# A fused two-block transformer kernel on one core: where the squares of the hidden layer stand in two engine queues, eight multiplications on another engine, and the order of a few loads and stores

## The chip, the cores and the metric

The program runs on one core of one Trainium2 chip. The metric is device time in microseconds (us) of one execution, as a median over runs; shorter is better.

## What is computed

The input x is 1024 tokens by 1024 features, float32. Three stages follow each other.

```python
# block 1: two layers, each x = x + rms_norm(mixer(rms_norm(x)))
#   layer 0: gmlp mixer (three 1024 x 2048 projections, 128-token spatial gating)
#   layer 1: dilated window attention, three groups of 16 heads
# block 2, on 1024 + 16 (meta) tokens:
#   h = rms_norm(x); z = h @ w_in
#   o = [stick-breaking attention | state-space scan (Ssd) | gated recurrence (Hgrn)]
#   x = x + o @ w_out
#   h = rms_norm(x)
#   u = relu(h @ w_up) ** 2
#   x = x + u @ w_down          # w_up: 1024 x 4096
```

The two recurrences work on chunks of 128 tokens and carry a state from one chunk to the next.

## The kernel before

Every large product is made three times on TensorE (PE), from operands that are split into an upper part (`hi`, rounded) and a rest (`lo`). ScalarE (ACT) makes `hi` (`split_hi`, L137), VectorE (DVE) makes `lo` (`split_lo`, L142), and PE then runs 24 matmuls for one weight unit of 1024 x 128 on 512 tokens (`products`, L155). SyncE (SP) loads the units into two raw buffers (L132). Each engine works through its own list of instructions in the order written; waits between engines are semaphores. GpSimd (POOL) mostly issues transfers.

**The last stage, `output_and_mlp`.** `units` is a list of 144 weight units: 8 of the output projection (positions 0 to 7), then for the first 512 tokens `up` and `down` in turn, 8 of each (up at positions 8 to 15, 24 to 31, 40 to 47, 56 to 63), the output projection of the second 512 tokens at 68 to 75, the rest of the first half, and last the same `up` and `down` units for the second 512 tokens. At each position n:

- PE: the recurrence phase n-1; wait for `lo` of unit n; wait until unit n-2 has left its bank; 24 matmuls into `z[n % 2]`.
- DVE: `split(n + 1)`; recurrence phase n-1; if unit n-1 was an up unit, `h_lo` of it (L4030); then the exit of unit n (for an up unit L4039: relu times the inverse norm, into `m[n % 2]`; for a down unit L4041: added to x).
- ACT: `split(n + 1)`, which waits until PE is done with unit n-1; recurrence phase n-1; `hidden(n - 1)`: if unit n-1 was an up unit, two squares of its `m` (L3924 `h_hi`, L3925 `y`).

The recurrence phases are 28 of `Ssd` (0 to 27: 4 chunks of 7), then 32 of `Hgrn` (28 to 59: 4 chunks of 8) and one last. Of an Hgrn chunk, phase 0 makes the gate's logarithms (ACT `mag`, `soft`; DVE sums to `cum`), phase 1 the distances (14 small DVE operations, L3751 and L3752), phase 2 their exponential on ACT (L3699) and on DVE `dq`, `dk` (L3760, L3761), `kend` (L3763) and `qe` (L3766). Phases 3 to 6 are scores on PE (L3648), which wait for `dq` and `dk`, and a masked sum on DVE; phase 7 gives the output. The chunk's inputs come to `raw` by `hg.load` (L3611 to L3616, two transfers from POOL's queue). `hg.load(0)` is issued at the stage's start; `sd.pool` stores each Ssd chunk's output (L2344) and ends with a wait for all four stores. The tile `dist` lies over the tile of Ssd's output, so DVE's first phase 1 waits for those stores (`ssd_stored`).

**The seam between attention and block 2.** x + y * norm * gain is made for the first 512 tokens at the end of `dilated_attention`, and for the second 512 at the start of `projection_and_sticks`, one 128-feature row k at a time. There DVE runs `scaled(k)` (L2978: m = y * inv), `add(k)` (L2982: x), `lower(k)` (L2988: the `lo` part) and for each two rows `pair` (L2994: the sum of two squares). ACT makes `hi` (L2716) and the square (L2718). PE runs 12 matmuls of row k for the first two weight units, and for each pair a matmul with ones (L2854) that sums over the features. In attention, `next_y(k)` (L2227), `next_x(k)` (L2233), `next_lower(k)` do the same, among DVE's `split_lo` of units that PE waits for (L1908).

**The stage boundary after the projection.** SP loads the first two units of w_out into the raw buffers, then stores the last projected unit (L2690). The next stage (`gated_recurrence`, the first Hgrn chunks) reads that unit.

Of the kernel before, what the change touches and what calls it, by code (L numbers as in the profile page):

```python
# [17 lines left out]
ACT = mybir.ActivationFunctionType  # L18
# [3 lines left out]
P = 128  # L22
# [1213 lines left out]
def dilated_attention(nc, shared, a_in, w, hi, lo, x_kept, yo, over_yo, over_w, blocks, inv, inv_post, x_out, bias_dram, o_dram, lse_dram, lead, lead_sum, ident,  # L1236
# [13 lines left out]
    with Stage(nc, "da") as st:  # L1250
# [246 lines left out]
        def _(pool):  # L1497
# [31 lines left out]
            for n in range(1, turns + 1):  # L1529
                turn(n)  # L1530

# [417 lines left out]
        def _(dve):  # L1949
# [272 lines left out]
            def next_y(k):  # L2222
                if k == 0:
                    dve.wait_ge(s_y, 16)
                    dve.wait_ge(s_ydone, 1)
                wait(dve, s_yx, k - 1)
                nc.vector.tensor_tensor(ym[k % 2], yo[:, k, halves[0]], inv_post[:, halves[0]], ALU.mult).then_inc(s_ym, 1)  # L2227

# [20 lines left out]
            for j in range(8, 24):  # L2249
                ahead = rows_of.get(j, ()) if j > 18 else ()  # L2250
                for k in ahead:
                    next_y(k)
# [7 lines left out]
                for k in rows_of.get(j, ()):  # L2260
                    if not ahead:
                        next_y(k)
# [251 lines left out]
def projection_and_sticks(nc, shared, mix_norms, late_out, a, w, hi, lo, inv, x, x_again, x_out, over_x, heads, hg, keep, table, cst, proj, conv, o_cat, ident, ones):  # L2514
# [31 lines left out]
    with Stage(nc, "pr") as st:  # L2546
# [19 lines left out]
        pairs = [total[:, 0:HALF], total[:, HALF:T]]  # L2566
# [24 lines left out]
        (s_par, s_table, s_m, s_xp, s_hi, s_lo, s_sq, s_pair, s_pmm, s_ln, s_inv, s_eps, s_zero, s_zout) = (  # L2591
            st.sem(n) for n in ("par", "table_in", "m_s", "xp", "hi_s", "lo_s", "sq_s", "pair", "pair_mm", "ln_s", "inv_s", "eps_s", "zero_s", "zero_out"))
# [29 lines left out]
        def _(sp):  # L2622
# [77 lines left out]
        def _(pool):  # L2700
            pool.wait_ge(s_zout, 48)
# [10 lines left out]
        def _(act):  # L2712
            nc.scalar.preload_act_table_set(EXP_LN)
            for k in range(KT):
                act.wait_ge(s_xp, k + 1)
                nc.scalar.activation(hi[:, k, late], x[:, k, late_in], ACT.Identity, scale=pre[:, k:k + 1]).then_inc(s_hi, 1)  # L2716
                wait(act, s_pair, k // 2)
# [3 lines left out]
            act.wait_ge(s_pmm, KT // 2)  # L2721
# [126 lines left out]
        def _(pe):  # L2848
            w.split(pe, 1, 0)
            w.products(begin[1][0][:, 0:PIECES[0][1]], 1, hi, lo, slice(*PIECES[0]))  # L2850

            def square_sum(p):
                pe.wait_ge(s_pair, p + 1)
                nc.tensor.matmul(pb[:, :], ones, pairs[p % 2], start=p == 0, stop=p == KT // 2 - 1).then_inc(s_pmm, 1)  # L2854

            for k in range(KT):
# [7 lines left out]
                if k and k % 2 == 0:  # L2864
                    square_sum(k // 2 - 1)
            square_sum(KT // 2 - 1)
# [103 lines left out]
        def _(dve):  # L2970
# [5 lines left out]
            def scaled(k):  # L2976
                wait(dve, s_xp, k - 1)
# [1248 lines left out]
```

## Time and profile before

| | |
|---|---|
| median of 3 runs | 3526.36 us (3518.29, 3526.36, 3527.9) |
| the profiled execution's own time | 3518.29 us |
| its span in the trace | 3516.5 us |
| mean granted TensorE clock | 0.994 of 2.4 GHz |
| busy, share of the span | PE 97%, DVE 61%, ACT 44%, POOL 3% |
| bytes moved | 315.8 MB, mean 90 GB/s |

Times in the trace are counted from the span's start. The seam lies at about 1971 to 2047, `gated_recurrence` at about 2545 to 2622, the last stage from 2623 to the end; its Hgrn phases begin at about 2819.

### The profile page before, as it was taken

To read this page: it belongs to the slowest core of one execution; us is meant where nothing else is said; L and a number is where in the kernel's file an instruction comes from. 1 tells how busy PE (TensorE), PEld (TensorE's weight loads), DVE (VectorE), ACT (ScalarE), POOL (GpSimd) and SP (SyncE) were. 2 spreads that over 40 slices of the span, in tenths; PEclk is the share of its full clock that TensorE was granted. 3 is DMA by queue.
4 is the path that set the end of the run, shared out by engine and by line. 5 is a ranking of instruction groups with operands and counts; after the bars stand their busy time and mean duration, and the time that the engine had idled before them with its cause. 6 is when DMAs were issued, how large, how long until landed. Compare 5 with 4: busy or idle time off the path is not lost. (4 is left out here: it accounts for less than half of the span.)

```text
span 3516.5 us, 48187 instructions
## 1 busy us (share of the span) xinstructions
PE 3420.0 (97%) x17584; PEld 2786.3 (79%) x17584; DVE 2153.6 (61%) x4253; ACT 1548.1 (44%) x3115; POOL 106.8 (3%) x143
## 2 busy tenths in 40 slices
PE   8999999989999999999999999999989999999999
PEld 6878887867777777777777788888878888878887
DVE  5477774575555566666778546776676577644333
ACT  4254443345444444544445546665334233332222
POOL 0000001000000000000000000000010000000000
PEclk9999999999999999999999999999989999999999
DMA  4232224621222122222223330122333222322223
GB/s 151 90 106 97 97 91 147 223 76 55 64 61 61 56 67 70 63 65 68 63 65 105 126 113 32 46 71 70 114 108 101 95 89 86 106 91 94 96 96 120
DMA packets 162201, 315.79 MB, mean 90 GB/s; under 512 B 33360, under 2 KB 78976, under 8 KB 161840
## 3 DMA queue, kind: packets, MB, share of 16 engines
q1 hardware_dynamic: 144048, 267.43, 23.0%
q0 software_dynamic: 15808, 36.89, 3.6%
q10 hardware_dynamic: 2112, 8.39, 0.6%
q8 instruction: 142, 2.33, 0.3%
q14 instruction: 91, 0.75, 0.1%
HBM read 259.69 MB, written 59.19 MB: 91 GB/s over the span
## 5 line engine op out<-in xcount | busy, mean ns | idle before, releaser
L137 ACT ACTIVATE all_w_hi<-all_w_raw 128x1024 fp32r<-128x1024 f32 x241 | 254.4, 1057 | 695.7 <-PE om_z L155 501.4
L142 DVE TENSOR_TENSOR all_w_lo<-all_w_raw,all_w_hi 128x1024 fp32r<-128x1024 f32 x241 | 294.9, 1224 | 246.2 <-ACT all_w_hi L137 245.9
L155 PE MATMUL om_z<-all_hi,all_w_hi 128*128 128x512 f32 x640 | 255.4, 399 | 3.3 <-PEq L45 2.0
L155 PE MATMUL om_z<-all_hi,all_w_lo 128*128 128x512 f32 x640 | 254.2, 397 | 0.0
L155 PE MATMUL om_z<-all_lo,all_w_hi 128*128 128x512 f32 x640 | 252.6, 395 | 0.0
L2128 DVE CUSTOM_DVE_ANT_0 at_logit<-da_qk,at_bias 128x256 f32<-128x256 f32 (+1 forms) x384 | 130.0, 376 | 164.3 <-issue 163.7
L1663 ACT ACTIVATE at_p<-at_logit,da_pair_max 128x256 f32<-128x256 f32 (+1 forms) x384 | 177.5, 465 | 100.3 <-DVE da_pair_max L2128 100.3
L155 PE MATMUL all_bank<-all_hi,all_w_hi 128*128 128x344 f32 (+1 forms) x632 | 215.3, 341 | 2.8 <-PEq L45 1.6
L1655 ACT ACTIVATE at_pt<-da_tr 128x512 f32<-128x512 f32 (+1 forms) x192 | 101.2, 527 | 263.6 <-PE da_tr L1855 263.5
L155 PE MATMUL om_z<-om_h_hi,all_w_hi 128*128 128x512 f32 x512 | 204.2, 399 | 2.1 <-DVE all_w_lo L142 1.6
L155 PE MATMUL all_bank<-all_hi,all_w_lo 128*128 128x344 f32 (+1 forms) x632 | 203.2, 322 | 0.0
L155 PE MATMUL all_bank<-all_lo,all_w_hi 128*128 128x344 f32 (+1 forms) x632 | 202.8, 321 | 0.0
L155 PE MATMUL om_z<-om_h_lo,all_w_hi 128*128 128x512 f32 x512 | 202.4, 395 | 0.0
L155 PE MATMUL om_z<-om_h_hi,all_w_lo 128*128 128x512 f32 x512 | 201.8, 394 | 0.0
L4041 DVE TENSOR_TENSOR all_yo<-all_yo,om_z 128x512 f32<-128x512 f32 x80 | 55.0, 688 | 194.2 <-PE om_z L155 194.1
L1865 PE MATMUL da_pv<-at_v,at_pt 128*128 128x64 f32 x1280 | 164.1, 267 | 0.0
L1865 PEld LDWEIGHTS da_pv<-at_v,at_pt 128*128 128x128 f32 x1280 | 159.8, 192 | 2.0
L2145 DVE TENSOR_TENSOR da_o<-da_pv,da_rden 128x128 f32<-128x128 f32 x192 | 56.0, 292 | 167.5 <-PE da_pv L1865 162.0
L1196 ACT ACTIVATE all_w_hi<-all_w_raw 128x512 fp32r<-128x512 f32 x190 | 118.3, 623 | 73.7 <-PE all_bank L1214 60.5
L155 PEld LDWEIGHTS om_z<-all_hi,all_w_hi 128*128 128x128 f32 x640 | 120.9, 189 | 32.3 <-issue 3.4
L155 PEld LDWEIGHTS om_z<-all_lo,all_w_hi 128*128 128x128 f32 x640 | 121.1, 189 | 27.5
L155 PEld LDWEIGHTS om_z<-all_hi,all_w_lo 128*128 128x128 f32 x640 | 120.8, 189 | 27.0
(815 smaller groups left out, 8757.0 us busy)
## 6 DMA issues: line engine op xcount, KB each, us to landing
all_w_raw<-in_w_mlp SPq DMA_DIRECT2D x128, 512.0 KB, 3.4
all_w_raw<-in_w_qkv SPq DMA_DIRECT2D x136, 256.0 KB, 2.7
all_w_raw<-in_w_ug SPq DMA_DIRECT2D x48, 512.0 KB, 4.2
all_w_raw<-in_w_in SPq DMA_DIRECT2D x27, 512.0 KB, 3.5
all_w_raw<-in_w_v SPq DMA_DIRECT2D x20, 512.0 KB, 4.4
vhat<-ag_vst ACTq DMA_DIRECT2D x4, 2048.0 KB, 7.4
ow_v<-vhat SPq DMA_DIRECT2D x16, 512.0 KB, 3.3
da_before<-o_groups POOLq DMA_DIRECT2D x32, 256.0 KB, 4.0
```

The source lines that it names most:

```text
L137: self.nc.scalar.activation(self.hi[b][:, :], self.raw[b][:, :], ACT.Copy).then_inc(self.hi_done[b], 1)
L142: self.nc.vector.tensor_tensor(self.lo[b][:, :], self.raw[b][:, :], self.hi[b][:, :].bitcast(F32), ALU.subtract).then_inc(self.lo_done[b], 1)
L155: last = self.nc.tensor.matmul(out, wp[b][:, w], ap[:, k, cols], start=(k == 0 and m == 0), stop=(k == KT - 1 and m == 2))
L1196: self.nc.scalar.activation(self.hi[n % self.slots], self.tile[name], ACT.Copy, scale=self.scales[j] if name in ("a11", "a12") else 1.0).t ...
L1655: nc.scalar.activation(pt[t % 2][:, 0:wd], tr[:, 0:wd], ACT.Copy).then_inc(s_pt, 1)
L1663: last = nc.scalar.activation(p[t % 2][:, hh, 0:wd], logit[t % 2][:, hh, 0:wd], ACT.Exp, scale=-1.0, bias=pair_max[:, t, hh:hh + 1], accum ...
L1865: last = nc.tensor.matmul(pv[:, 64 * hh:64 * hh + 64], pt[t % 2][:, i * P:i * P + P], v[:, t + x, 64 * hh:64 * hh + 64], start=(x == 0), s ...
L2128: last = nc.vector.tensor_tensor_reduce(out=logit[t % 2][:, hh, 0:wd], in0=qk[hh][:, 0:wd], in1=bias[ag][hh][x][:, :], scale=1.0, scalar=3 ...
L2145: nc.vector.tensor_tensor(o[:, t, :].rearrange("p (h c) -> p h c", h=2), pv[:, 0:P].rearrange("p (h c) -> p h c", h=2), rden[:, t, :].rear ...
L4041: nc.vector.tensor_tensor(x[:, i, halves[h]], x[:, i, halves[h]], z[b][:, :], ALU.add).then_inc(s_ev, 1)
```

## The change

Four groups of edits.

1. In the last stage ACT's two squares of an up unit move from position n + 1 to the end of position n, where they wait for the exit of that unit; they now stand ahead of `split(n + 2)`. On DVE, `h_lo` of the unit before moves ahead of `split(n + 1)` and the recurrence phase.
2. `hg.load(0)` is issued after `sd.pool`, not at the stage's start; the wait `ssd_stored` goes. In Hgrn's phase 2, `kend` and `qe` come ahead of `dq` and `dk`.
3. At both parts of the seam the product y * inv (8 rows of 128x512 each) goes from DVE to POOL. At the second part the sums of squares are no longer added in pairs with 4 matmuls but gathered by 7 DVE operations into one tile, with one matmul at the end.
4. SP stores the last projected unit before it loads the two units of w_out, not after.

```diff
@@ dilated_attention, gpsimd, after its turns
+            pool.wait_ge(s_y, 16)
+            pool.wait_ge(s_ydone, 1)
+            for k in range(KT):
+                wait(pool, s_yx, k - 1)
+                nc.gpsimd.tensor_tensor(ym[k % 2], yo[:, k, halves[0]], inv_post[:, halves[0]], ALU.mult).then_inc(s_ym, 1)
@@ dilated_attention, vector: next_y(k), the same product, and its calls go
-                nc.vector.tensor_tensor(ym[k % 2], yo[:, k, halves[0]], inv_post[:, halves[0]], ALU.mult).then_inc(s_ym, 1)
@@ projection_and_sticks, sync
+            sp.wait_ge(s_ev, 3 * NU)
+            sp.dma_start(proj[units[NU - 1]][:, P - META:], ev[(NU - 1) % 3][:, TAPS - 1:]).then_inc(late_out, 16)
             sp.wait_ge(h_next, 32)
             w.load(sp, 0, 14, a["w_out2"][0])
             w.load(sp, 1, 13, a["w_out2"][1])
-            sp.wait_ge(s_ev, 3 * NU)
-            sp.dma_start(proj[units[NU - 1]][:, P - META:], ev[(NU - 1) % 3][:, TAPS - 1:]).then_inc(late_out, 16)
@@ projection_and_sticks, gpsimd
+            for k in range(KT):
+                wait(pool, s_xp, k - 1)
+                nc.gpsimd.tensor_tensor(m[k % 2], x[:, k, late_in], inv[:, late], ALU.mult).then_inc(s_m, 1)
@@ projection_and_sticks, tensor: the four square_sum(p) go
+            pe.wait_ge(s_acc0, KT - 1)
+            nc.tensor.matmul(pb[:, :], ones, total[:, late], start=True, stop=True).then_inc(s_tot, 1)
@@ projection_and_sticks, vector
-            scaled(0)
-            scaled(1)
             add(0)
-            for k in range(KT):
-                if k + 2 < KT:
-                    scaled(k + 2)
+            lower(0)
+            add(1)
+            for k in range(1, KT):
                 if k + 1 < KT:
                     add(k + 1)
                 lower(k)
-                if k % 2:
-                    pair(k // 2)
+                gather(k)
+            def gather(k):
+                dve.wait_ge(s_sq, k + 1)
+                t = total[:, late]
+                if k == 1:
+                    nc.vector.scalar_tensor_tensor(t, sq[0], 1.0, sq[1], ALU.mult, ALU.add).then_inc(s_acc0, 1)
+                else:
+                    dve.wait_ge(s_acc0, k - 1)
+                    nc.vector.scalar_tensor_tensor(t, t, 1.0, sq[k % 2], ALU.mult, ALU.add).then_inc(s_acc0, 1)
@@ Hgrn.pool and Hgrn.dve
+        self.load(pool, 0)
-            if i == 0:
-                dve.wait_ge(*self.ssd_stored)
-            dve.wait_ge(self.s_ed, i + 1)
-            nc.vector.tensor_tensor(t["dq"], ...)
-            nc.vector.tensor_tensor(t["dk"], ...).then_inc(self.s_dqk, 1)
             dve.wait_ge(self.s_end, i + 1)
             nc.vector.tensor_tensor(t["kend"], ...)
             nc.vector.tensor_tensor(t["qe"], ...)
+            dve.wait_ge(self.s_ed, i + 1)
+            nc.vector.tensor_tensor(t["dq"], ...)
+            nc.vector.tensor_tensor(t["dk"], ...).then_inc(self.s_dqk, 1)
@@ output_and_mlp, gpsimd
-            hg.load(pool, 0)
             sd.pool(pool)
             hg.pool(pool)
@@ output_and_mlp, scalar
                 split(n + 1)
                 recurrences(lambda r: r.act, act, n - 1)
-                hidden(n - 1)
...
+                if kind == "up":
+                    act.wait_ge(s_ev, n + 1)
+                    wait(act, s_hl, ups(u) - 1)
+                    nc.scalar.activation(h_hi[:, i, :], m[n % 2][:, :], ACT.Square)
+                    nc.scalar.activation(y[n % 2][:, :], m[n % 2][:, :], ACT.Square).then_inc(s_hh, 1)
@@ output_and_mlp, vector
-                split(n + 1)
-                recurrences(lambda r: r.dve, dve, n - 1)
                 if n and units[n - 1][0] == "up":
                     v = units[n - 1]
                     dve.wait_ge(s_hh, ups(v) + 1)
                     nc.vector.tensor_tensor(h_lo[:, v[3], :], y[(n - 1) % 2][:, :], h_hi[:, v[3], :].bitcast(F32), ALU.subtract).then_inc(s_hl, 1)
+                split(n + 1)
+                recurrences(lambda r: r.dve, dve, n - 1)
```

## Rows read from the trace of the kernel before

**Rows 1.** The page: busy us (share of the span) xinstructions.

```profile
PE 3420.0 (97%) x17584; PEld 2786.3 (79%) x17584; DVE 2153.6 (61%) x4253; ACT 1548.1 (44%) x3115; POOL 106.8 (3%) x143
```

**Rows 2.** PE's waits, 2623 to 3516: waiter <- releaser: us, times, longest.

```profile
PE om_two L3648 <- DVE x_kept L3761: 3.5, 4, 0.9
...
PE om_z L155 <- DVE om_h_lo L4030: 0.5, 1, 0.5
```

**Rows 3.** The chain that ended last, 2806 to 2838: start, us, what.

```profile
2806.98 22.31 PE om_z L155 x96
...
2836.14 2.05 PE om_two L3648 x16
```

**Rows 4.** ACT's timeline, 2818 to 2832: start, us, instruction [idle before].

```profile
2818.25 1.06 ACT L137 ACTIVATE all_w_hi<-all_w_raw 128x1024 fp32r<-128x1024 f32 x1 [2.09 <-PE om_z L155]
...
2820.94 0.62 ACT L3925 ACTIVATE om_y<-om_m 128x512 f32<-128x512 f32 x1
...
2830.34 1.69 ACT L3699 ACTIVATE hi_f<-hi_f 128x1792 f32<-128x1792 f32 x1
```

**Rows 5.** DVE's timeline, 2815 to 2833.

```profile
2815.87 0.69 DVE L2480 TENSOR_TENSOR hi_f<-hi_f,mixers_gn 128x512 f32<-128x512 f32 x1
...
2819.34 1.23 DVE L142 TENSOR_TENSOR all_w_lo<-all_w_raw,all_w_hi 128x1024 fp32r<-128x1024 f32 x1 [0.46 <-ACT all_w_hi L137]
2820.54 0.43 DVE L3731 SCALAR_TENSOR_TENSOR x_kept<-om_raw,x_kept 128x256 f32<-128x256 f32 x1
...
2822.32 0.67 DVE L4030 TENSOR_TENSOR om_h_lo<-om_y,om_h_hi 128x512 fp32r<-128x512 f32 x1
2823.75 0.69 DVE L4039 SCALAR_TENSOR_TENSOR om_m<-om_z,all_inv 128x512 f32<-128x512 f32 x1 [0.76 <-PE om_z L155]
...
2826.04 0.28 DVE L3751 TENSOR_TENSOR hi_f<-x_kept 128x128 f32<-128x128 f32 x1
...
2828.87 0.69 DVE L4030 TENSOR_TENSOR om_h_lo<-om_y,om_h_hi 128x512 fp32r<-128x512 f32 x1
...
2832.12 2.03 DVE L3760 TENSOR_TENSOR hi_f<-hi_f,om_raw 128x1792 f32<-128x1792 f32 x1 [0.43 <-ACT hi_f L3699]
```

**Rows 6.** Transfers, 2500 to 3070: KB each, median us from issue to landing.

```profile
om_raw<-proj POOLq DMA_DIRECT2D x8, 256.0 KB, 4.8
...
o_cat<-hi_f POOLq DMA_DIRECT2D x4, 256.0 KB, 2.5
```

**Rows 7.** POOL's timeline at the start of the last stage.

```profile
2625.53 1.48 POOL L3616 DMA_DIRECT2D om_raw<-proj  x2
```

**Rows 8.** POOL's timeline in the stage before the last.

```profile
2580.11 1.98 POOL L3330 TENSOR_TENSOR hg_gg<-hg_gate,mixers_hg_gn 128x256 f32<-128x256 f32 x1 [8.22 <-ACT hg_gate L3398]
2585.61 0.73 POOL L3333 TENSOR_TENSOR x_kept<-hg_o,hg_gg 128x256 f32<-128x256 f32 x1 [3.53 <-ACT hg_o L3367]
```

**Rows 9.** DVE's timeline at the same time.

```profile
2579.48 2.02 DVE L3533 TENSOR_TENSOR hg_dq<-hg_dist,hp_raw 128x1792 f32<-128x1792 f32 x1
2581.42 2.55 DVE L3535 TENSOR_TENSOR hg_dk<-hg_dist,hp_key 128x1792 f32<-128x1792 f32 x1
```

**Rows 10.** Lines of the seam: count, ns min/median/max, first and last start.

```profile
L2982 DVE SCALAR_TENSOR_TENSOR all_yo<-pr_big,mixers_post,da_y x8: 744/745/748, 2023.7 to 2037.8; 128x512 f32<-128x512 f32 x8
...
L2854 PE MATMUL pr_pb<-pr_total,all_ones x8: 590/591/592, 2033.0 to 2045.4; 128*128 128x512 f32 x8
```

**Rows 11.** Waits, 1970 to 2050.

```profile
PE all_bank L1908 <- DVE all_w_lo L142: 2.4, 2, 1.5
```

**Rows 12.** SP's timeline ahead of the stage boundary.

```profile
2525.84 1.18 SPq L132 DMA_DIRECT2D all_w_raw<-in_w_out  x2
...
2542.78 0.33 SPq L2690 DMA_DIRECT2D proj<-pr_ev  x1
```

**Rows 13.** PE's waits, 2094 to 2101.

```profile
PE pr_pb L2903 <- ACT pr_ce L2746: 2.3, 1, 2.3
```

**Rows 14.** The stretch right behind that wait: length, PE, PEld, DVE, ACT, POOL busy, clock, DMA.

```profile
2097.30:2100.70 3.40, 3.40 (x12) 2.90 (x12) 0.10 (x1) 0.56 (x1) 0.00 (x0) 0.57 0.00 0
```

More of the change, by code:

```diff
@@ L2974, in _ @@
             sd.dve_start(dve)
-            def scaled(k):
-                wait(dve, s_xp, k - 1)
-                nc.vector.tensor_tensor(m[k % 2], x[:, k, late_in], inv[:, late], ALU.mult).then_inc(s_m, 1)
             def add(k):
@@ L2989, in lower @@
                                                ALU.mult, ALU.subtract).then_inc(s_lo, 1)
-            def pair(p):
-                dve.wait_ge(s_sq, 2 * p + 2)
-                wait(dve, s_pmm, p - 1)
-                nc.vector.tensor_tensor(pairs[p % 2], sq[0], sq[1], ALU.add).then_inc(s_pair, 1)
-            scaled(0)
-            scaled(1)
+            def gather(k):
[6 more added lines that the diff above has]
+                    nc.vector.scalar_tensor_tensor(t, t, 1.0, sq[k % 2], ALU.mult, ALU.add).then_inc(s_acc0, 1)
             add(0)
-            for k in range(KT):
-                if k + 2 < KT:
-                    scaled(k + 2)
+            lower(0)
+            add(1)
+            for k in range(1, KT):
                 if k + 1 < KT:
@@ L3598, with __init__ @@
     PHASES = 8
[L3600 to L3601 removed]
+    def __init__(self, st, proj, o_cat, keep, tile, bank, cst, first, count):
         self.nc, self.proj, self.o_cat, self.first, self.count = st.nc, proj, o_cat, first, count
@@ L3758, in dve @@
                 link(nc.vector.memset(t["key"][:, :, 0:P - META], 0.0))
-            dve.wait_ge(self.s_ed, i + 1)
-            nc.vector.tensor_tensor(t["dq"], t["dist"], over(t["raw"][:, 0:2, :]), ALU.mult)
-            nc.vector.tensor_tensor(t["dk"], t["dist"], over(t["key"]), ALU.mult).then_inc(self.s_dqk, 1)
             dve.wait_ge(self.s_end, i + 1)
@@ L3766, in dve @@
             nc.vector.tensor_tensor(t["qe"], t["ecum"], t["raw"][:, 0:2, :], ALU.mult).then_inc(self.s_qe, 1)
+            dve.wait_ge(self.s_ed, i + 1)
+            nc.vector.tensor_tensor(t["dq"], t["dist"], over(t["raw"][:, 0:2, :]), ALU.mult)
+            nc.vector.tensor_tensor(t["dk"], t["dist"], over(t["key"]), ALU.mult).then_inc(self.s_dqk, 1)
         if ph in (3, 4, 5, 6):
@@ L3843, in output_and_mlp @@
         sd = Ssd(st, proj, conv, o_cat, keep, sd_tile, (bank[0], bank[1], bank[2:4], bank[5]), cst, first, count)
-        hg = Hgrn(st, proj, o_cat, keep, hg_tile, (two[:, :], bank[2], bank[3], bank[4][:, 0:2 * P], bank[4][:, 2 * P:]), cst, first, count,
-                  (sd.s_left, 16 * count))
+        hg = Hgrn(st, proj, o_cat, keep, hg_tile, (two[:, :], bank[2], bank[3], bank[4][:, 0:2 * P], bank[4][:, 2 * P:]), cst, first, count)
         s_o = st.sems("o_in", tiles // 2)
@@ L3916, in scale @@
                     nc.scalar.activation(hi[:, c, halves[h]], x[:, c, halves[h]], ACT.Identity, scale=gain[:, c:c + 1]).then_inc(s_hi2, 1)
-            def hidden(n):
-                u = units[n]
-                if n < 0 or u[0] != "up":
-                    return
-                act.wait_ge(s_ev, n + 1)
-                wait(act, s_hl, ups(u) - 1)
-                nc.scalar.activation(h_hi[:, u[3], :], m[n % 2][:, :], ACT.Square)
-                nc.scalar.activation(y[n % 2][:, :], m[n % 2][:, :], ACT.Square).then_inc(s_hh, 1)
             act.wait_ge(s_gain, 16)
```

27 lines of the change are left out of this document (5 added, 22 removed).

## Prediction

> **What bounds the kernel now.** First the page's line of busy times [rows 1]: PE is busy for 97% of the span, so DVE or ACT work costs nothing while it stays behind PE's matmuls, and an edit can gain only where PE waits. So next PE's waits in the last stage [rows 2]: over 893 us only a handful of us, 3.5 of them at four places, the scores of a gated-recurrence chunk waiting for `dk`. One more, 0.5, is PE at a first down unit waiting for the `h_lo` of the last up unit. The chain [rows 3] gives PE's pace: 96 matmuls, four units, in 22.31 us, so 5.58 per unit; they end at 2829.29. It also shows the place where the stage is tight: the scores start only at 2836.14, when `dk` is ready. The timelines of ACT and DVE around it [rows 4, 5] give the durations for the walk below. The seam and the clock are read further down, with their edits.
>
> **Squares ahead of the next split (edit 1).** Call P the end of unit n on PE. Before, `split_hi(n + 2)` starts at P: `hi` 1.06, `lo` 1.23, with the exit and the squares behind them. `lo` is ready 2.4 after P, and PE wants it 5.6 after P. Now the exit comes first, 0.69, then the two squares, about 1.15 (0.62 is one, the pair overlaps), then `hi` 1.06, `lo` 1.23 [rows 4, 5]. With the starts between them, `lo(n + 2)` is ready at P + 4.2. That is still inside 5.6: without recurrence work the edit is free, so in the second half of the tokens it costs nothing. With recurrence work of length R on DVE a loop closes: exit, squares, `hi`, `lo`, R, next exit, 4.15 + R per unit. PE's own period is 5.58 plus what the phase puts on PE. R by Hgrn phase, from DVE's starts [rows 5]: phase 0 1.78 in the first chunk (2820.54 to 2822.32), about 3.0 later (three more such operations of 0.43 for the output of the chunk before); phase 1 2.83 (2826.04 to 2828.87); phase 2 4.0 for `dq` and `dk` (2832.12 to 2836.14) and about 0.7 for `kend` and `qe`, the shape of the 0.43 row. PE adds almost nothing in phases 0 to 2, and over 2 us in phases 3 to 6 (2.05 the scores [rows 3]); there the loop of about 7.4 stays under PE's 7.6 and more. Ssd's phases have R of 2.1 at most (three operations of 0.69): loop 6.2 at worst against 5.9, absorbed by the 1.4 of slack. So the loss is in phases 0 to 2, where they meet up units: chunk 0 (phases 28 to 30, up to position 31) and chunk 2 (44 to 46). Chunks 1 and 3 meet down units, whose exits don't pass ACT.
>
> The walk, from P of the unit before phase 0. Before, `dk` is ready at P + 18.0: in chunk 0 P is 2829.29 - 11.15 = 2818.1 and PE starts the scores at 2836.14. Now in chunk 2: exit 0.7, squares 1.9, `hi` 2.95, `lo` 4.2, phase 0 7.2, exit 7.9, `lo` 11.3, phase 1 14.2, exit 14.9, `lo` 18.3, `kend` and `qe` 19.0 (`exp` of 1.69 on ACT is ready by then), `dq` and `dk` 22.9. That is **4.9 us** late, and PE stands for it: what is queued behind PE's wait are the scores and all products after them, so nothing is caught up. In chunk 0 without edit 2 the same walk with R 1.78 gives 21.7, 3.7 late. `h_lo` ahead of the split takes away the 0.5 [rows 2]: -0.5.
>
> **The late load (edit 2).** Ssd's last output leaves DVE at 2816.56 [rows 5], by the loop some 1.5 later: 2818.1. The store lands 2.5 after its issue, and 0.3 is taken for the hand-over: 2820.9. Then POOL issues two transfers, 1.48 in sum, and the second lands 4.8 after its issue [rows 6, 7]: 2826.5, P + 8.4. ACT has been at phase 0 since P + 3, and behind it on ACT stand the squares of unit 29 and `hi` of unit 31. From 8.4: three small ACT operations 1.2 (from the end of `hi` to 2820.54 [rows 4, 5]) 9.6, phase 0 11.4, exit 12.1, `lo(31)` 15.5. PE wants that at 11.6 and stands for 3.9. Then phase 1 18.4, exit 19.1, `lo` 22.5, `kend` and `qe` 23.2, `dk` 27.1 or a little more: **9.3 us** after 18.0. That takes in the 3.9 and the 3.7. If the raw data had landed by P + 3, edit 2 would be free. In chunks 1 and 3, `kend` and `qe` first cost 0.7 less the 0.43 that DVE waited for the exponential [rows 5]: 0.25 each, **0.5**.
>
> **The products on POOL (edit 3).** No row has 128x512 on POOL. The same operation on 128x256 took 0.73 alone; another took 1.98, having started while DVE ran a product of two SBUF operands (2579.48 to 2581.50) and ended 0.6 after it [rows 8, 9]. And DVE's next such product took 2.55 where 2.02 is its length: 0.53 longer. So each waits for the other. For 128x512 I take twice that, 1.06 of DVE time per product; bounds 0 and 1.46 (twice 0.73). The Trainium skill states this as a rule (SBUF — State Buffer, Who interferes with whom): a VectorE instruction with two SBUF inputs and a GpSimd instruction that reads SBUF exclude each other for the whole instruction; the trace agrees, with 0.53 us. By the Trainium skill (GPSIMD Engine Reference, 3.1 Elementwise) a two-input fp32 operation on 2048 elements takes 4497 ns; a quarter, 1.12 us, is an estimate from that page, and the sum would be 0.4 more by it.
>
> Second part of the seam, stage start: `m(0)` is about on time: POOL needs 1.46 at most, and two DVE products of 0.69 stood ahead of the first `add`, at 2023.7 [rows 10]. Up to the end of `lower(7)` DVE has 22 operations (8 add, 8 lower, 6 gather) of 0.745 less the 0.08 by which neighbours overlap (2579.48 + 2.02 against 2581.42 [rows 9]), 14.6, and 7 blocks of 1.06, 7.4: 2045.7. PE then has 12 matmuls of the last row, about 1.9 (0.232 [rows 3] x 344/512 x 12), and the one matmul with ones. Before, its last one starts its second half at 2045.4 [rows 10]. Now about 2047.9: **+2.5**. Lower bound: no lock, PE paces itself and saves three matmuls with ones (about 0.45 each in PE's order): -1.5. Upper: 7 x 0.4 more, +5.3. First part: 8 products of 0.69 leave DVE's queue, where PE waits 2.4 for `split_lo` [rows 11], but 8 blocks of 1.06 come in, partly in idle time: taken as **0**, bounds -2.4 (both waits go) and +5.
>
> **Store before the loads (edit 4).** The loads were issued 17 us ahead [rows 12] and now follow the store: their 1.18 of issue ends at 2544.3, past the store's 2543.1, so the stage boundary moves a little, and the first loads of the next stage queue behind 1 MB: **+0.5**, bounds 0 and 2.
>
> **The clock.** A PE wait of 2.3 us was followed by 3.4 us at a mean granted clock of 0.57 [rows 13, 14], so 1.2 GHz for most of it: 3.4 x 0.43 = 1.5 us lost. Chunks 0 and 2 now have waits of over 5 us each in front of PE-bound work: **3.0** in sum (the earlier wait of 3.9 in chunk 0 may have one too, but its loss is inside the wait for `dk`). Bounds 0 and 6.
>
> **Sum.** 9.3 + 4.9 + 0.5 - 0.5 + 3.0 + 2.5 + 0 + 0.5 = 20.2. On the profiled execution's own 3518.29 (1.8 more than its span): 3538.5. That execution is the fastest of three and 8.1 below the median; on the median 3526.36 the forecast is 3546.6, **3547**. 0.3% is 10.6 us, about what a measurement of this kernel can tell from no change.
>
> **Rivals.** (a) *The load is hidden*: store and transfers land sooner than the medians, or phase 0's wait is made up. Against it: 8.4 against 3 is far. Then chunk 0 costs 3.7, not 9.3, in sum 14.6: 3541. (b) *The lock costs a whole POOL product each time, at both parts of the seam*: +5.3 and +5 in place of 2.5 and 0, and a clock drop at PE's waits there, 1.5: 3556. This is the case that the Trainium skill's rule of exclusion (SBUF — State Buffer, Who interferes with whom) names. For it: two rows of exclusion; against: DVE has idle time at the first part. (c) *Not slower*: PE's gain at the seam is all that shows. The squares' loop never closes, because `m` leaves early enough that DVE's phase always runs under PE's unit, and the seam loses its waits. It gives -2.4 - 1.5 - 0.5: 3522, no change. It decides if the loop is 5.6 or less, R under 1.4; phases 1 and 2 have 2.83 and 4.7, so little speaks for it. (d) *Loop smaller, clock kept*: a mix of (a) and no drops, 3538 or less.
>
> **Chances.** The forecast 0.55, (a) 0.15, (b) 0.13, (c) 0.08, (d) 0.09. Its own range is 3541 to 3553. The asked one reaches to (d) and (b): 3531 to 3561. Slower by over 0.3% (above 3537): 0.55 + 0.15 + 0.13 and part of (d), 0.86. Faster by over 0.3% needs 10.6 us and the gains sum to 4.4: 0.03. Within: 0.11.
>
> **What the changed profile would show.** PE's waits: `om_two L3648 <- DVE` at two of four chunks longer, about 5 each, at the others about 1.2; one wait of about 4 for `lo` of unit 31. ACT idle for 5 us before `mag` of chunk 0, released by a DMA. In the second half of the tokens no new wait, `split_hi` 2 us behind PE's end. Half-clock stretches behind the long waits. At the seam POOL products of 1.3 to 2 us, DVE's add and lower stretched to 1.8 in turn, and PE waiting for `lower`. The prediction is wrong if the scores start on time, if PE waits in up units without recurrence work, or if the stage boundary or the attention part moves by several us.

## The result and the profile after

The changed kernel takes 3550.44 us, the median of four runs (3547.98 to 3554.9), against 3524.62 for four runs of the kernel before (3518.29 to 3527.9). The ratio is 1.0079, with a 95% interval of 1.0066 to 1.0092: it is slower by 0.8%, some 26 us. The forecast was 3547, with a range of 3531 to 3561. The profiled execution took 3550.18, its span 3548.4, at a mean granted clock of 0.988 (0.994 before).

The page's line of busy times of the changed kernel, to be set against [rows 1]:

```profile
PE 3432.9 (97%) x17578; PEld 2796.8 (79%) x17578; DVE 2161.7 (61%) x4240; ACT 1548.5 (44%) x3115; POOL 133.3 (4%) x159
```

PE has 6 matmul records fewer and is busy 13 us longer: the work hasn't grown, so part of it ran at a lower clock. The rest of the 32 us between the two spans must be PE standing. Its waits in the last stage of the changed kernel (waiter <- releaser: us, times, longest), the counterpart of [rows 2]. Line numbers differ a little between kernels: L3636 here is L3648 there, the scores, and `x_kept L3752` is `dk`.

```profile
PE om_two L3636 <- DVE x_kept L3752: 11.6, 4, 5.4
PE om_z L155 <- DVE all_w_lo L142: 6.1, 2, 4.5
```

The wait for `dk` has grown from 3.5 to 11.6 us. The wait for a weight's `lo` is new but for 1.6 of it, a wait at another place that the kernel before has too. The wait for `h_lo` is gone. PE's timeline around chunk 0, where unit 31 and then the scores start, the counterpart of the last row of [rows 3]:

```profile
2842.94 0.80 PE L155 MATMUL om_z<-all_hi,all_w_hi 128*128 128x512 f32 x1 [4.52 <-DVE all_w_lo L142]
2854.30 3.35 PE L3636 MATMUL om_two<-hi_f,x_kept 64*128 64x128 f32 x14 [4.08 <-DVE x_kept L3752]
```

How these two waits come about can be followed in the chain of the same stretch (start, us, what), which carries Ssd's last output, its store, the load, and DVE's and ACT's work on the chunk:

```profile
2826.28 0.70 DVE hi_f L2474
2826.99 0.28 issue
2827.27 2.50 DMA o_cat<-hi_f
2829.77 0.28 issue
2830.05 0.75 POOL om_raw L3603
2830.81 4.87 DMA om_raw<-proj
2835.70 0.43 ACT x_kept L3668
...
2838.91 0.59 DVE om_m L4018
...
2840.06 0.61 ACT om_y L3922
2840.68 0.96 ACT all_w_hi L137
2841.63 0.02 issue
2841.66 1.23 DVE all_w_lo L142
...
2850.29 2.02 DVE hi_f L3751
2852.31 1.95 DVE x_kept L3752
```

With P, the end of unit 28 on PE, at 2826.9 (DVE's exit starts there), the raw data is in at P + 8.8, `lo` of unit 31 at P + 16.0, and `dk` at P + 27.4, where it was P + 18.0 before.

The price of the clock is best read from the same piece of PE's work at each chunk, from the scores' first matmul to the first matmul of the second unit behind them (about 62 records). These are the windows of the kernel before (window, its length, PE busy, mean granted clock, DMA share, GB/s), and under them those of the changed kernel:

```profile
2836.10:2846.40 10.30, 10.26 (x61) 1.00 0.15 52
2892.20:2902.60 10.40, 10.37 (x62) 1.00 0.16 52
2948.80:2959.10 10.30, 10.30 (x63) 1.00 0.15 52
3004.90:3015.30 10.40, 10.38 (x63) 1.00 0.15 50
```

```profile
2854.30:2868.70 14.40, 14.40 (x61) 0.69 0.10 36
2914.70:2925.10 10.40, 10.38 (x63) 1.00 0.15 53
2975.80:2989.30 13.50, 13.50 (x63) 0.75 0.12 40
3035.20:3047.10 11.90, 11.88 (x61) 0.86 0.14 44
```

PE doesn't stand in any of these windows, and yet the first takes 4.1 us longer than before, the third 3.2, the fourth 1.5. 10.3 of work at full speed, with the clock at 1.2 GHz for part of the time, gives nearly these lengths (14.4 x 0.69 = 9.9, 13.5 x 0.75 = 10.1). That is 8.9 us of clock behind the four waits (8.8 by the rounded lengths), where the kernel before lost nothing in its profiled execution. Of this, 7.3 stand behind the two long waits and 1.6 behind the one of 1.1 us at chunk 3.

Where the 31.9 us between the two spans lie, by the positions of PE's first matmuls on both timelines: 3.6 just ahead of the seam, where the changed code has not yet been reached and where all other kernels below are late by 2.5 to 6.7 us too (the profiled execution of the kernel before was a quick one there); 0.1 in the first part of the seam; 3.3 in the second; 3.3 from there to the last stage, 1.0 of it at the boundary where the store now stands first; 21.6 in the last stage (893.1 before, 914.7 now). The other 2.3 of that 3.3 can't be put down to the change: the kernels below that have no edit there take 0.7 to 3.4 longer than the kernel before's profiled execution on the same stretch. So about 26 of the 31.9 are the change's.

### The profile page after: what moved, and what is told of

The parts are those of the page before. It is cut to its first block and busy times, and to the rows that moved or that the text cites. A ratio compares the mean times of both kernels' runs of the same rounds, so it can differ in the third digit from the quotient of the medians.

```text
span 3548.4 us, 48180 instructions
## 1 busy us (share of the span) xinstructions
PE 3432.9 (97%) x17578; PEld 2796.8 (79%) x17578; DVE 2161.7 (61%) x4240; ACT 1548.5 (44%) x3115; POOL 133.3 (4%) x159
## 5 line engine op out<-in xcount | busy, mean ns | idle before, releaser
L3921 ACT ACTIVATE om_h_hi<-om_m 128x512 fp32r<-128x512 f32 x64 | 40.4, 631 | 247.8 <-DVE om_m L4018 247.8
L155 PEld LDWEIGHTS om_z<-all_lo,all_w_hi 128*128 128x128 f32 x640 | 121.5, 190 | 27.7
```

The source lines that it names most:

```text
L155: last = self.nc.tensor.matmul(out, wp[b][:, w], ap[:, k, cols], start=(k == 0 and m == 0), stop=(k == KT - 1 and m == 2))
L3921: nc.scalar.activation(h_hi[:, i, :], m[n % 2][:, :], ACT.Square)
```

## The experiments

Each ran beside the kernel before. Besides the ratio of its times I read the length of its last stage and the four windows at the chunks, which leave out what differs in earlier stages. They come from one profiled execution each. A difference of single microseconds can't be had from the times alone.

### One part at a time: the squares, the load

`squares_alone` is the kernel before with edit 1 (squares at the end of position n on ACT, `h_lo` ahead of the split on DVE) and nothing else.

> The kernel before with edit 1 alone (squares of an up unit ahead of the next split on ACT, h_lo ahead of it on DVE). By the walk of the prediction: dk of chunk 0 is 3.7 us later, dk of chunk 2 4.2 us later (4.9 less the 0.7 of kend and qe, which stay behind dk here), chunks 1 and 3 unchanged, 0.75 back at the first down units (what the trace of the changed kernel showed; 0.5 was predicted), and behind the two longer waits of PE a clock loss. With the predicted 1.5 each the whole is +10.2 us; with the 3 to 4 each that the changed kernel showed it is +13 to +15. Rival (the squares cost nothing by themselves, the load does it all): 0 to +1 us, and no wait of PE for dk over 2 us.

Measured: ratio 1.0043, interval 1.0031 to 1.0056, so +15 us; last stage 908.0, +14.9. Its waits of PE in the last stage:

```profile
PE om_two L3648 <- DVE x_kept L3761: 11.2, 4, 5.3
```

The four waits for `dk` are 4.1, 0.9, 5.3 and 0.9: 3.2 and 4.4 longer at chunks 0 and 2, unchanged at 1 and 3, as the walk said. That is 7.6 of waits. About 1.4 came back ahead of chunk 0: 0.8 by `h_lo` and 0.6 that every kernel but one has against the profiled execution of before (the start of the stage ran a little quicker). The four windows take 14.2, 10.4, 13.5 and 11.9, which is 8.7 of clock, and 7.6 - 1.4 + 8.7 is the 14.9. Of the 8.7, 1.6 stand behind a wait of 0.9 at chunk 3 that the kernel before has too. The rival falls.

`load_alone` has the load and the dropped wait of edit 2, and before's order of `kend`, `qe`, `dq`, `dk`:

```diff
     def pool(self, pool):
+        self.load(pool, 0)
         for i in range(self.count):
...
-            if i == 0:
-                dve.wait_ge(*self.ssd_stored)
...
-            hg.load(pool, 0)
             sd.pool(pool)
```

> The kernel before with the load of Hgrn's first chunk behind Ssd's last store, and the wait for that store at the distances gone (edit 2 without the order of kend and qe). The raw data lands at about the same time after the start of the phase, less the 1.5 us by which the squares' loop delays Ssd's last output: about 7 us after the end of the unit before phase 0. Phase 0 then starts some 4 us late, but without the closed loop DVE and ACT can make up for it: the lo of unit 31 is wanted at 11.6 and ready at about 14, so PE waits 2.5 there, and dk of chunk 0 is 3.5 to 5.5 us late in all. With 1.5 to 3 of clock: +5 to +8 us. Chunks 1 to 3 as before. Rival (the load costs something only together with the late squares): under +1.5 us, no wait for lo, and dk of chunk 0 within 1 us of before.

Measured: 1.0021, interval 1.0011 to 1.003; last stage 904.8, +11.7. PE waits 1.6 for `lo` of unit 31 and 3.2 for `dk` of chunk 0, and the scores are 3.8 us later from the stage's start. So the waits are as expected, and the load costs by itself. The ratio is some 7 us, inside the 5 to 8 that I gave; the last stage of the profiled execution, which was one of the slower of eleven (3536.2, their median 3531.6), is above it, by the clock, at chunks that the edit doesn't reach:

```profile
2846.20:2859.60 13.40, 13.40 (x62) 0.75 0.11 40
2905.40:2917.30 11.90, 11.86 (x61) 0.86 0.14 45
2963.50:2975.40 11.90, 11.89 (x63) 0.86 0.13 45
3021.20:3033.10 11.90, 11.90 (x61) 0.86 0.14 44
```

These windows lose 3.1, 1.5, 1.6 and 1.6. The last three stand behind PE waits of 0.9, 0.85 and 0.9, which the kernel before has too [rows 2], with a clock of 1.00 behind them in its profile. So those 4.7 are no price of the load; without them the last stage would be 7.0 longer, as the ratio has it.

`changed_load_early` is the changed kernel with the load back at the start of the stage and the wait for Ssd's store back at the distances.

> The changed kernel with the load of Hgrn's first chunk at the start of the stage again and the wait for Ssd's store back at the distances. The wait for lo of unit 31 (4.5 us in the changed kernel) goes, dk of chunk 0 comes 3.7 late instead of 9.5, chunk 2 stays at +4.5. Waits shrink by 5.8 us; if the clock loss in chunk 0 (3.9) hangs on the sum of the two waits, up to 2 more come back. So 6 to 8 us less than the changed kernel: 3542 to 3545 us in its terms, +0.4% to +0.6% on the kernel before. Rival (the load is not what delays unit 31): no difference from the changed kernel.

Measured: 1.0065, interval 1.0052 to 1.0078, median 3549.1; last stage 908.2, which is 6.5 less than in the changed kernel. The wait for `lo` of unit 31 is gone and the scores of chunk 0 start 6.0 earlier from the stage's start (5.6 was the prediction's difference of 9.3 and 3.7). The windows take 14.1, 10.4, 13.4 and 11.9: the clock still costs 8.4, so it did not hang on the sum of the two waits of chunk 0. (In the changed kernel the clock is low at the start of unit 31 as well, behind the wait of 4.5: its matmuls start 0.43 us apart for the first 3 us and 0.23 apart later. These 1.5 us are over before `dk` is ready, as the prediction said.) The median is above the range I gave. The two ratios differ by 0.0014, 5 us, and their intervals overlap, so it is the trace that gives the size; the whole spans of the two profiled executions differ by 1.1 only, as this one reached the last stage 5.4 later.

### The clock behind a wait of known length

`dk_later` is the kernel before with more `dq` products on DVE, one in chunk 0, two, three and four in the next:

```diff
+            for k in range(i + 1):
+                nc.vector.tensor_tensor(t["dq"], t["dist"], over(t["raw"][:, 0:2, :]), ALU.mult).then_inc(self.s_more, 1)
+                dve.wait_ge(self.s_more, i * (i + 1) // 2 + k + 1)
             nc.vector.tensor_tensor(t["dq"], t["dist"], over(t["raw"][:, 0:2, :]), ALU.mult)
```

> The kernel before, with 1, 2, 3 and 4 additional dq products on DVE (about 2.0 us each, of the same data) ahead of dq in chunks 0, 1, 2 and 3: a measure of the clock behind a wait of known length. PE's waits for dk become about 2 to 3, 5, 8 and 9 us; 20 us are added to the span by the waits themselves (PE has nothing else to do). What is above 20 is the clock's. Theory: each wait of over 4 us is followed by a stretch at half clock that costs 1.5 to 4 us, so three or four of them: +26 to +34 us in sum. If the price does not grow with the wait, chunks 1, 2 and 3 lose the same. Rival (half-clock stretches come anyway, whatever PE waits for): +20 us, and the clock rows as before.

Measured: 1.0098, interval 1.0084 to 1.0112; last stage 924.9, +31.8. PE's waits for `dk` became 2.9, 5.0, 7.0 and 9.2. Their windows, in the same order:

```profile
2843.50:2855.30 11.80, 11.80 (x62) 0.86 0.14 46
2905.20:2919.40 14.20, 14.17 (x62) 0.71 0.11 38
2971.80:2985.20 13.40, 13.40 (x63) 0.75 0.11 40
3039.20:3053.00 13.80, 13.77 (x62) 0.73 0.13 38
```

The waits add 20.6 (24.1 in sum for 3.5) and the clock 1.5 + 3.8 + 3.1 + 3.4 = 11.8, less the 0.6 at the stage's start. A wait of 2.9 us cost 1.5 behind it; waits of 5, 7 and 9 us cost 3 to 4 each, no more for the longer. That is the theory's case, and by the ratio at its upper part. The waits of the changed kernel fit in: 4.1 (behind 4.5 a little earlier) brought 4.1, 5.4 brought 3.2. The run also shows that every microsecond by which DVE is late for `dk` is a microsecond of the end: nothing is caught up.

The windows of all fourteen kernels show where this is sure and where it is chance. Each number is the window's length less 10.3 (10.4 at chunks 1 and 3), good to 0.1, with PE's wait ahead of it in brackets; the last three kernels are told of further down:

```
                     chunk 0     chunk 1     chunk 2     chunk 3
before               0   (0.9)   0   (0.9)   0   (0.9)   0   (0.9)
store_first          0   (0.9)   0   (0.9)   0   (0.9)   0   (0.9)
seam_first           0   (0.9)   1.5 (0.9)   1.6 (0.9)   0   (0.9)
second_gather        0   (0.9)   1.5 (0.9)   1.6 (0.9)   0   (0.9)
load_alone           3.1 (3.2)   1.5 (0.9)   1.6 (0.9)   1.6 (0.9)
squares_alone        3.9 (4.1)   0   (0.9)   3.2 (5.3)   1.5 (0.9)
changed_load_early   3.8 (4.2)   0   (1.1)   3.0 (5.4)   1.5 (1.1)
changed kernel       4.1 (4.1)   0   (1.1)   3.2 (5.4)   1.5 (1.1)
dk_later             1.5 (2.9)   3.8 (5.0)   3.1 (7.0)   3.4 (9.2)
seam_second          0   (0.9)   1.5 (0.9)   1.6 (0.9)   0   (0.9)
second_pool_pairs    0   (0.9)   1.5 (0.9)   1.6 (0.9)   0   (0.9)
changed_chunk_ahead  3.2 (2.8)   0   (0)     3.8 (4.2)   0   (0)
chunk_ahead_of_split clock 1.00 in all four, no wait for dk
best                 clock 1.00 in all four, no wait for dk
```

A wait of about 1 us was followed by a loss of 1.5 or 1.6 in 14 of the 33 cases of this table, a wait of 2.8 us or more by 1.5 to 4.1 in all 13, and no wait by none in all 10. The length alone doesn't set the price: 2.8 in `changed_chunk_ahead` brought 3.2, and 2.9 in `dk_later` 1.5. Nor does a short wait cost anything everywhere: the 1.6 for a `lo` later in the last stage, which all fourteen kernels have, is followed by a clock of 1.00 in each. What differs at the chunks is the work behind the wait, the small score matmuls and not a unit's; whether that is what counts no run here has tested.

### The seam: products on POOL, the chain of sums

`seam_first` has only the first eight products on POOL.

> The kernel before with only the first 8 products of y and inv on POOL (edit 3, first part of the seam, in the attention stage). Prediction 0, bounds -2.4 and +5; the changed kernel's trace put DVE's next weight split 3.6 us later, and 3.6 also stood ahead of it before the seam, so 0 is expected: ratio 1.000. Rival (b): each product on POOL blocks DVE for its length of 1.3 us where DVE was on the path: up to +5 us, to be seen as PE's waits for split_lo there growing from 2.4 to over 5.

Measured: 0.9993, interval 0.9984 to 1.0001. From PE's first matmul of the seam (1970.3 before, 1974.0 here) to the first one of the next stage it takes 52.1 us, 52.0 before. The waits for `split_lo` are 1.5 and 1.0, where they were 1.5 and 0.9. The products, alone 1.28 us long, are stretched up to 2.2 where DVE is at work, and so is DVE's operation beside them:

```profile
1989.56 2.23 POOL L1535 TENSOR_TENSOR da_k_even<-all_yo,all_inv 128x512 f32<-128x512 f32 x1 [2.78 <-DVE all_yo L2231]
1990.56 1.78 DVE L2237 SCALAR_TENSOR_TENSOR all_lo<-all_yo,mixers_pre,all_hi 128x512 fp32r<-128x512 f32 x1
```

Three of the eight products ran while DVE had nothing of this kind to do. Five collided, and each held one operation of 0.68 or 0.74 for 1.78: 5.3 us in sum, against about 5 that the eight products had taken of DVE before (0.60 to 0.72 from start to start). In a stretch of 38.3 us DVE is busy for 29.7, where it was 29.0. No cost: the 0 of the prediction holds, and rival (b) falls in this part.

`seam_second` has the second part: products on POOL, chain of seven sums, one matmul with ones.

> The kernel before with only the second part of edit 3: 8 products on POOL, the chain of seven sums on DVE and one matmul with ones in place of four. By the changed kernel's trace +3.3 us at the first exit behind it (2.5 was predicted) and about that at the end: +2.5 to +4 us, ratio 1.0007 to 1.0012. Rival: PE paces this part and it costs nothing or gains 1.5.

Measured: 1.0009, interval 1.0 to 1.0018. From PE's first matmul of the stage to the first one behind the matmuls with ones: 27.7 us, 24.4 before, +3.3. POOL's and DVE's timelines in the changed kernel, which has the same code here, show how they collide:

```profile
2036.41 1.73 POOL L2696 TENSOR_TENSOR pr_big<-all_yo,all_inv 128x512 f32<-128x512 f32 x1 [1.29 <-DVE all_yo L2969]
2039.42 1.73 POOL L2696 TENSOR_TENSOR pr_big<-all_yo,all_inv 128x512 f32<-128x512 f32 x1 [1.29 <-DVE all_yo L2969]
```

```profile
2035.59 0.74 DVE L2969 SCALAR_TENSOR_TENSOR all_yo<-pr_big,mixers_post,da_y 128x512 f32<-128x512 f32 x1
2036.25 0.74 DVE L2975 SCALAR_TENSOR_TENSOR all_lo<-all_yo,mixers_pre,all_hi 128x512 fp32r<-128x512 f32 x1
2036.91 1.77 DVE L2985 SCALAR_TENSOR_TENSOR pr_total<-pr_total,pr_big 128x512 f32<-128x512 f32 x1
2038.61 0.74 DVE L2969 SCALAR_TENSOR_TENSOR all_yo<-pr_big,mixers_post,da_y 128x512 f32<-128x512 f32 x1
```

The product is released at 2036.4 by the end of `add`, while `lower` runs; it ends at 2038.1, 1.2 after `lower` did. The sum that starts at 2036.9 takes 1.77 where the same sum takes 0.69 elsewhere, and ends 0.5 after the product: little of it was done when the product was. So a row costs three operations and one block, 3.02 us (2035.59 to 2038.61), and PE, which needs 1.9 per row, waits:

```profile
PE all_bank L155 <- DVE all_lo L2975: 5.2, 6, 0.9
```

Two variants take the part apart. `second_pool_pairs` keeps before's pair sums and its four matmuls and moves only the products:

```diff
-            scaled(0)
-            scaled(1)
             add(0)
             for k in range(KT):
-                if k + 2 < KT:
-                    scaled(k + 2)
                 if k + 1 < KT:
                     add(k + 1)
                 lower(k)
                 if k % 2:
                     pair(k // 2)
```

> As seam_second, but only the products move to POOL; the four pair sums and four matmuls with ones stay. If the exclusion between DVE's two-input operations and POOL's products is the cost, this has it too: 20 DVE operations of 0.745 less 0.08, 13.3, and 7 times 1.06, 7.4, so the last lower is 2 us earlier than in seam_second, and the stage comes within 0 to +1.5 us of before. Rival (the lock costs nothing, the chain with its late single matmul is what costs): -2 us, DVE 8 operations shorter.

`second_gather` keeps the products on DVE, in before's places, and has the chain of seven sums and the one matmul:

> As seam_second, but the 8 products stay on DVE; only the chain of seven sums and the single matmul are new. DVE has 3 more operations of 0.69 to 0.75 than before (2.1 us), PE three matmuls with ones fewer (0.45 each, 1.4). If DVE paces: +2 us; if the sums lie beside PE: 0. No operation of DVE is stretched to 1.78. Rival (single chain is the whole cost of seam_second): +3.3 us.

Measured: `second_pool_pairs` 1.0008 (0.9999 to 1.0017), the part takes 27.4 us, +3.0; `second_gather` 1.0003 (0.9995 to 1.0012), the part takes 23.8 us, -0.6. The times can't separate these; the traces do. In `second_gather` no operation of DVE is stretched, and a row of four costs less than a row of three with a product on POOL beside it (start to start of the first of these lines, and the like one a row later at 2034.78, 2.53 us):

```profile
2032.25 0.69 DVE L2992 TENSOR_TENSOR pr_big<-all_yo,all_inv 128x512 f32<-128x512 f32 x1
2032.85 0.75 DVE L2972 SCALAR_TENSOR_TENSOR all_yo<-pr_big,mixers_post,da_y 128x512 f32<-128x512 f32 x1
2033.52 0.75 DVE L2978 SCALAR_TENSOR_TENSOR all_lo<-all_yo,mixers_pre,all_hi 128x512 fp32r<-128x512 f32 x1
2034.18 0.69 DVE L2988 SCALAR_TENSOR_TENSOR pr_total<-pr_total,pr_big 128x512 f32<-128x512 f32 x1
```

So moving the products to POOL costs 3.0 of the 3.3 of this part. The chain of sums gains 0.6 with the products on DVE and costs 0.3 on top of the products on POOL, where each sum is one more operation that stands behind a product. I had expected 0 to +1.5 from the one and 0 to +2 from the other, and missed both. For the first I had only counted DVE's time up to the last `lower`. In its trace PE waits 1.5 for the first `lower`, where it waits 0.1 in the kernel before; its blocks hold up the early `lower` on which PE's row depends. I take this for the reason, but no run has it alone.

### The store ahead of the loads

```diff
+            sp.wait_ge(s_ev, 3 * NU)
+            sp.dma_start(proj[units[NU - 1]][:, P - META:], ev[(NU - 1) % 3][:, TAPS - 1:]).then_inc(late_out, 16)
             sp.wait_ge(h_next, 32)
             w.load(sp, 0, 14, a["w_out2"][0])
             w.load(sp, 1, 13, a["w_out2"][1])
```

> The kernel before with edit 4 alone, the last projected unit's store ahead of the two w_out2 loads. Predicted +0.5 us, bounds 0 and 2; in the changed kernel's trace PE's idle time at the start of the next stage was 1.0 us longer (6.9 for 5.9) and the chunk's start on SP 1.06 later. So +0.5 to +1 us between the last matmul of the projections and the first one of the last stage; ratio 1.000. Rival: the first loads queue behind the 1 MB and the stage starts over 2 us late.

Measured: 1.0, interval 0.9991 to 1.0009. SP's timeline and PE's wait at the start of the next stage:

```profile
2549.66 0.33 SPq L2687 DMA_DIRECT2D proj<-pr_ev  x1
2550.09 1.21 SPq L132 DMA_DIRECT2D all_w_raw<-in_w_out  x2
2553.47 0.34 SPq L3301 DMA_DIRECT2D mixers_hg_gn<-in_hg_gain  x1
```

```profile
PE hg_sc L3418 <- PEq L45: 6.9, 1, 6.9
```

In the kernel before the stage's first load on SP came 2.7 us after the store of [rows 12], now 3.8, and PE's wait at the boundary was 5.9. So the boundary comes 1.0 us later, nearly the 1.2 that the issue of the loads takes, and from there to the last stage's first matmul it is 78.7, for 77.8 before and 79.6 in `seam_first`: the loads themselves aren't late.

### What to do with the order around dk

The closed loop suggests its own mending: at phase 2 let ACT and DVE do the chunk's work first and the weight split after it, since PE has the scores' 2.05 us [rows 3] to do between this unit and the next.

```diff
+                early = is_p2(n - 1)
+                if early:
+                    recurrences(lambda r: r.dve, dve, n - 1)
                 split(n + 1)
-                recurrences(lambda r: r.dve, dve, n - 1)
+                if not early:
+                    recurrences(lambda r: r.dve, dve, n - 1)
```

The same on ACT; `is_p2` is true for phase 2 of each chunk.

> The kernel before, but at phase 2 of each of the four chunks ACT and DVE do the recurrence's work (exponential of the distances, dq, dk) ahead of the next weight split. Before, PE waited 0.85 to 0.92 for dk at every chunk. hi (1.06) and lo (1.23) leave the path to dk; the exponential can start when the distances are there, about 0.5 earlier, so dk is 0.5 to 1 us earlier. Its four waits of PE go, and with them what half-clock stretches they bring: -2 to -3.5 us from the waits, and up to 3 more if stretches of 1.5 came behind waits of 0.9 in executions of the kernel before (one alone had none, those of the two seam kernels had two each). Ratio 0.9985 to 0.9993. Rival: lo now comes late for the unit behind the scores, a new wait of 1 us or more on PE at each chunk, and nothing is gained.

Measured: 0.9986, interval 0.9977 to 0.9995, -5 us; last stage 889.6, -3.5. PE waits for `dk` nowhere, there is no new wait for `lo`, and the windows at the chunks are all at a clock of 1.00. Of the h_lo waits there are now three, 1.1 us in sum, for one of 0.5. The same edit on the changed kernel:

> The changed kernel with phase 2 of each chunk ahead of the next split, as in chunk_ahead_of_split. If the wait for dk is the end of a closed loop of exits, squares, hi, lo and phase on two engines, taking hi and lo (2.3 us, with ACT's hi partly beside it 1.2) out of its last turn makes dk 1.2 to 2.3 us earlier in every chunk: PE's waits for dk from 4.1, 1.1, 5.4, 1.1 to about 2.5, 0, 3.6, 0. With clock losses that do not shrink at the two long ones that is 5 to 6 us less than the changed kernel, +0.6% on before; if they shrink too, +0.5%. Rival: PE then waits for lo of the next unit instead, and the time stays.

Measured: 1.005, interval 1.0038 to 1.0063, median 3543.6, 6.8 below the changed kernel's (10 by the ratios, whose intervals lie just apart); last stage 908.2, -6.5.

```profile
PE om_two L3636 <- DVE x_kept L3752: 7.1, 2, 4.2
PE om_z L155 <- DVE all_w_lo L142: 6.0, 2, 4.5
```

The waits for `dk` are 2.8 and 4.2 at chunks 0 and 2, none at 1 and 3: 1.1 to 1.25 us off at each of the four. So `hi` and `lo` were part of the path to `dk`, as the loop has it, and what is left is the rest of the loop.

`best` is `chunk_ahead_of_split` and `second_gather` together, with edit 1 kept only for the last up unit ahead of the down units:

```diff
+                if last_up(u):
+                    hidden(n)
```

> A version made of what gained: chunk_ahead_of_split; the chain of seven sums with one matmul at the second part of the seam, with the products on DVE (second_gather gained 0.6 us between the stage's start and the units behind it); and the squares of edit 1 ahead of the next split only for the last up unit before a down unit, where PE waited 0.5 for h_lo and no recurrence phase follows on an up unit. Sum: -0.6 - 0.7 - 2 to -3.5, and the clock as for chunk_ahead_of_split: -3.5 to -7 us, ratio 0.998 to 0.999. Rival: only the noise of the clock is left, 1.000.

Measured: 3519.68 us, 0.9978, interval 0.9968 to 0.9987, so 7.5 us below the kernel before. Last stage 887.1, -6.0. No wait for `dk` or `h_lo` is left in it, and its windows at the chunks:

```profile
2837.90:2848.00 10.10, 10.10 (x61) 1.00 0.32 104
2893.00:2903.20 10.20, 10.20 (x61) 1.00 0.35 104
```

The edit that cost 15 us for all units takes away the waits for `h_lo` (0.5 before, 1.1 in `chunk_ahead_of_split`) when it is made at the one up unit in eight that stands ahead of a down unit. No run has it alone; the last stage is 2.5 shorter than that of `chunk_ahead_of_split`, and 0.7 of this lies at the stage's start.

## Why the prediction was right, and where its sizes were off

The result was called by sign and nearly by size (3547 for 3550.4), and it went the way that the walk described. The added time was further off than these two numbers: 20.2 in the sum, 25.8 between the medians and 27.8 by the ratio. The forecast stood on 3526.36 for the kernel before, and its median in the comparison was 3524.62; that brought the two times 1.7 nearer to each other and is luck.

- **Chunk 0, 9.3.** Measured 9.4 (`dk` at P + 27.4 instead of P + 18.0). Inside it, the raw data at P + 8.8 for 8.4, `lo(31)` at P + 16.0 for 15.5, PE's wait there 4.5 for 3.9. The division into 3.7 for the loop and the rest for the load holds: `squares_alone` has 3.2, `changed_load_early` wins back 6.0. Rival (a) falls.
- **Chunk 2, 4.9.** Measured 4.6 in the changed kernel; 4.4 in `squares_alone`, which has no `kend` and `qe` ahead of `dk`. So these two cost 0.2 here, where the walk gave them 0.7, and the rest of the loop was a little longer than its 4.2. **Chunks 1 and 3, 0.25 each**: 0.15 each.
- **h_lo, -0.5.** The wait is gone. The positions of the units ahead of chunk 0 give about 0.8.
- **The clock, 3.0.** This is the term that was mis-sized, by a factor of three: 8.9 in the changed kernel's trace, 7.3 of it at the two places that the prediction counted. I had taken the row behind a wait of 2.3 us, with 1.5 lost, as the price of a wait of 5 as well [rows 13, 14], and had counted only two places. `dk_later` has 1.5 behind a wait of 2.9, and 3.1 to 3.8 behind 5 to 9, and other kernels have 3.1 and 3.2 behind waits of 3.2 and 2.8; and a wait of 1 us, which I had at nothing, has 1.5 behind it in some executions. The upper bound of 6 was too low as well. Some of it isn't the change's: the kernel before, too, may lose 3.1 at chunks 1 and 2 in some executions, as the four seam kernels, which don't touch that stage, do in their profiles. So the sum of the measured terms (27) may well stand a little above the difference of the medians (26).
- **Second part of the seam, 2.5.** Measured 3.3. The block per collision was 1.06 in the sum; a sum of 0.69 took 1.77, 1.08 more, and an `add` of 0.74 took 1.76. `lower(7)` ended at 2045.6 on the clock of the kernel before, for 2045.7 predicted. What was short is PE behind it: the last rows were released faster than PE works them off (the last three `lower` end at 2046.05, 2047.98 and 2049.24, and PE needs 1.9 per row), so the last row was done 0.7 later than predicted. The Trainium skill (SBUF — State Buffer, Who interferes with whom) calls what such instructions of the two engines contend for an exclusive lock; the traces agree nearly: product and `lower` follow each other to 0.1 us (1.15 of the product's 1.28 lie behind it), and of the sum's 0.69 the last 0.5 lie behind the product. By the Trainium skill (GPSIMD Engine Reference, 3.1 Elementwise) the product was estimated at 1.12 us; it took 1.28.
- **First part of the seam, 0.** Measured 0.1, ratio of `seam_first` 0.9993. Only five of eight products collided, and what they cost DVE was what it had got rid of. Rival (b) needed both parts, and a loss of clock at PE's waits there; the changed kernel's six waits of 0.9 at the second part are followed by a clock of 1.00. It falls.
- **The store, 0.5.** Measured 1.0, at the boundary itself and nowhere later.
- **Rival (c)** needed the loop to stay under PE's unit; the waits for `dk` in `squares_alone` refute it. **Rival (d)** needed the clock to stay.

The terms as measured: 9.4 + 4.6 + 0.3 - 0.8 + 8.9 + 3.3 + 0.1 + 1.0 = 26.8.

The parts don't add up one by one, and the experiments say how. The waits are more than the sum of the two edits: 3.2 and 4.0 (1.6 and 2.4) of `squares_alone` and `load_alone` at chunk 0, but 9.4 together: the late load adds 6.0 to the kernel that has the longer loop and 4.0 to the one that hasn't. The clock is less than the sum (8.7 and 7.9 alone, 8.9 together); but 4.7 of `load_alone` and 1.6 of `squares_alone` stand behind waits of 0.9 that neither edit made, and what is left is 7.1, 3.2 and, together, 7.3, since both edits lose it at chunk 0.

## What to carry to other kernels

Work moved ahead of a weight split is free only while the whole round (exit, moved work, split, what the recurrence adds) stays shorter than PE's unit; write the round down for each phase before moving anything, and move it only at the positions that have room. Price a PE wait with what comes behind it: here a wait of 5 us cost 8 to 9. An elementwise product moved to GpSimd beside a vector engine that works on two SBUF operands without a pause costs more than it takes away: here 1.06 us for each that collided, against 0.6 that it had taken. Where the vector engine has gaps for some of them, the two can cancel.

## What the runs showed of the hardware

- PE's granted clock fell behind waits of 0.9 us at the chunks in some profiles (14 of 33 cases), in a kernel in which PE is busy for 97%, and not in others whose last stage is the same code. It did not fall behind waits of 0.9 at the seam, nor behind one of 1.6 in the last stage. I had thought it took a longer wait. What decides it stays open: the experiments changed lengths of waits, not their position in time or the work behind them.
- Behind waits of 5, 7 and 9 us the loss was the same within a microsecond (3.8, 3.1, 3.4).
- A VectorE sum of two SBUF operands that was issued while a GpSimd product ran took 1.77 us instead of 0.69, and the product 1.73 to 2.23 instead of 1.28: each stood for the other.
- The profiled execution of the kernel before stood 2.5 to 6.7 us ahead of all 13 others at the start of the seam, which no edit has reached yet. Without the median beside it, its span would have given all experiments that much too much.
